# Three passes over rounded parts for the embedding projections of a two-layer decoder step

## What is computed

```python
def run(x, p, sample):
    ...
    for i in range(DEPTH):
        ...
        x = x + rms_norm(m, norm_g[i, 1])
        f = squared_relu_mlp(rms_norm(x, norm_g[i, 2]), w_ff1[i], w_ff2[i])
        x = x + rms_norm(f, norm_g[i, 3])
        gate = jax.nn.sigmoid(x @ w_ple_gate[i] + b_ple_gate[i])
        x = x + gate * (p[i] @ w_ple[i])
```

## Time and profile before

| | |
|---|---|
| runs | 1772.66, 1778.82, 1775.17 us; median 1775.17 us |
| the profiled execution's own time | 1768.82 us |
| its span, first to last instruction | 1767.0 us |
| mean granted clock of TensorE | 0.984 of full |
| PE busy | 1687.0 us, 95% |
| DVE, ACT, POOL busy | 753.2, 621.1, 604.1 us |
| projection's products (L743) | 128 records, 32.4 us busy |
| weight splits on ACT and POOL | 98 each, mean 1907 and 4626 ns |

### The profile page before, as it was taken

One profiled execution on the slowest core, in us unless ns is written; L12 is line 12 of the kernel. 1 busy time (PEld: TensorE's weight loads), 2 busy tenths in 40 slices (PEclk: granted clock), 3 DMA queues, 4 the chain that ended last, 5 costly groups with the idle time before them and its releaser, 6 DMA issues.

```text
span 1767.0 us, 31043 instructions
## 1 busy us (share of the span) xinstructions
PE 1687.0 (95%) x13335; PEld 1575.5 (89%) x13335; DVE 753.2 (43%) x1101; ACT 621.1 (35%) x968; POOL 604.1 (34%) x286
## 2 busy tenths in 40 slices
PE   6999999899999999998999878999799999999998
PEld 6998879799999999997999545668799999999988
DVE  4999953520212112265054757884340111312252
ACT  4211145432322223244222446875343231413232
POOL 3551322233333333322342003665324343333312
PEclk9999999899999999998999998999999999999999
DMA  7229703133322222121336881001212222122212
GB/s 255 80 93 163 240 1 144 72 113 126 131 109 76 93 72 96 48 96 66 91 95 194 290 275 49 2 1 62 96 49 72 80 88 96 72 96 72 84 60 78
DMA packets 61338, 180.07 MB, mean 102 GB/s; under 512 B 22914, under 2 KB 23826, under 8 KB 47314
## 3 DMA queue, kind: packets, MB, share of 16 engines
q1 hardware_dynamic: 60530, 177.18, 30.2%
q10 hardware_dynamic: 128, 0.88, 0.3%
q0 software_dynamic: 544, 0.03, 0.0%
HBM read 167.02 MB, written 16.45 MB: 104 GB/s over the span
## 4 chain that ended last, share of the span: by engine, by line
PE 76%; DVE 15%; ACT 3%; issue 2%; SPq 1%; DMA 1%; POOL 1%; ACTq 0%; DVEq 0%; POOLq 0%
PE ps L691 21%; PE ps L693 21%; PE ps L692 21%; DVE ps L1655 8%; PE ps L1090 2%; PE ps L1080 2%; PE ps L813 2%; PE ps L1107 2%; DVE big L1637 1%; POOL w_lo L615 1%; PE ps L926 1%; DVE hb L1541 1%; ACT w_hi L1147 1%; SPq L531 1%; DVE x L1604 1%
## 5 line engine op out<-in xcount | busy, mean ns | idle before, releaser
L615 POOL TENSOR_TENSOR w_lo<-w_raw,w_hi 128x2048 fp32r<-128x2048 f32 x98 | 453.3, 4626 | 853.5 <-ACT w_hi L1147 853.5
L691 PE MATMUL ps<-ha,w_hi 128*128 128x288 f32 x1920 | 572.4, 298 | 16.5 <-DVE hb L1612 9.1
L692 PE MATMUL ps<-hb,w_hi 128*128 128x288 f32 x1920 | 569.0, 296 | 0.0
L693 PE MATMUL ps<-ha,w_lo 128*128 128x288 f32 x1920 | 568.7, 296 | 0.0
L691 PEld LDWEIGHTS ps<-ha,w_hi 128*128 128x128 f32 x1920 | 363.2, 189 | 23.7 <-issue 17.7
L693 PEld LDWEIGHTS ps<-ha,w_lo 128*128 128x128 f32 x1920 | 363.8, 189 | 0.0
L692 PEld LDWEIGHTS ps<-hb,w_hi 128*128 128x128 f32 x1920 | 363.7, 189 | 0.0
L691 PE MATMUL ps<-hid_hi,w_hi 128*128 128x288 f32 x1024 | 301.8, 295 | 0.0
L693 PE MATMUL ps<-hid_hi,w_lo 128*128 128x288 f32 x1024 | 301.7, 295 | 0.0
L692 PE MATMUL ps<-hid_lo,w_hi 128*128 128x288 f32 x1024 | 301.6, 295 | 0.0
L1147 ACT ACTIVATE w_hi<-w_raw 128x2048 fp32r<-128x2048 f32 x98 | 186.9, 1907 | 174.7 <-PE ps L693 165.1
(11 more groups left out here) (250 smaller groups left out, 1985.0 us busy)
## 6 DMA issues: line engine op xcount, KB each, us to landing
w_raw<-in_w SPq DMA_DIRECT2D x98, 1024.0 KB, 4.8
ring<-in_sel_pages SPq DMA_DIRECT2D x64, 256.0 KB, 3.8
ring<-in_cmp_pages SPq DMA_DIRECT2D x40, 256.0 KB, 4.3
attn_t<-in_win SPq DMA_DIRECT2D x16, 512.0 KB, 7.1
cmp_hb<-in_cmp_pages SPq DMA_DIRECT2D x16, 256.0 KB, 4.3
x<-in_x SPq DMA_DIRECT2D x4, 576.0 KB, 5.9
out_y<-x SPq DMA_DIRECT2D x8, 288.0 KB, 2.1
big<-in_cmp_pages SPq DMA_DIRECT2D x8, 256.0 KB, 4.0
```

Of the source, the lines that this page charges most:

```text
L615: nc.gpsimd.tensor_tensor(w_lo[j % 2][:, :], w_raw[:, k, :], w_hi[j % 2][:, :].bitcast(F32), ALU.subtract).then_inc(w_ready, 1)
L691: nc.tensor.matmul(to, wh, chunk(hi, k, a * HT, HT), start=k == 0, stop=False)
L692: nc.tensor.matmul(to, wh, chunk(lo, k, a * HT, HT), start=False, stop=False)
L693: return nc.tensor.matmul(to, wl, chunk(hi, k, a * HT, HT), start=False, stop=k == C - 1)
```

## The change

The projection's weights become one more stage of the weights' list ("ple0", "ple1", one block each), so that they are split like all others. The embedding input is split into `ple_hi` (ScalarE) and `ple_lo` (VectorE, in place of `ple_in`) in the third quarter of the MLP. TensorE makes 12 products a tile in place of 4. As the helper `tile` now splits the projection's block where it split the gate's first one, and does not act in the projection's own tiles, the gate's first block is split by a call of its own in ScalarE's `ple`, after the copies of tiles 0 and 1. The numbers of the blocks after the projection move by one, so their parity does, and the places in the ring that the attention's transfers use are swapped with them.

```diff
-W_STAGES = ([("pw1", 8), ("pw2", 4)] + [(s, 4) for s, _, _ in mlp_stages(0)] + [("gate0", 4), ("q", 4), ("kv_cmp", 2),
-            ("k_rot", 2), ("v_tok", 2), ("out", 4)] + [(s, 4) for s, _, _ in mlp_stages(1)] + [("gate1", 4)])
+W_STAGES = ([("pw1", 8), ("pw2", 4)] + [(s, 4) for s, _, _ in mlp_stages(0)] + [("ple0", 1), ("gate0", 4), ("q", 4), ("kv_cmp", 2),
+            ("k_rot", 2), ("v_tok", 2), ("out", 4)] + [(s, 4) for s, _, _ in mlp_stages(1)] + [("ple1", 1), ("gate1", 4)])
...
-    _per = TT if _s == "v_tok" else 2
+    _per = TT if _s == "v_tok" else C if _s.startswith("ple") else 2
...
-    if _s.startswith("gate"):
-        BLOCKS.append(("ple", int(_s[-1])))
...
     elif _src == "w1":
-        PLACE.append((BLK, 9))
+        PLACE.append((2 * BLK, 9))
     elif _src == "sel_pages":
-        PLACE.append((BLK * ((_row + 2) % 3), 2 + (_row + 2) % 3))
+        PLACE.append((BLK * (1, 0, 2)[_row % 3], 2 + (1, 0, 2)[_row % 3]))
...
                     if was == "w":
                         sp.wait_ge(w_ready, n + 1)
-                    elif was == "ple":
-                        sp.wait_ge(tile_done, FIRST[f"ple{n}"] + C)
...
             def ple(layer, norm):
 
-                i = B_OF["ple", layer]
-                block_there(i)
-                pe.wait_ge(ple_loaded, 16 * (layer + 1))
-                w = w_raw[:, PLACE[i][1], :].rearrange("p (k c) -> p k c", k=2)
+                j = W_OF[f"ple{layer}"]
+                pe.wait_ge(w_ready, j + 1)
+                pe.wait_ge(ple_split, layer + 1)
+                wh, wl = (w[j % 2].rearrange("p (k c) -> p k c", k=2) for w in (w_hi, w_lo))
...
                         for k in range(2):
-                            last = nc.tensor.matmul(slot(t)[:, a, :], w[:, k, m * P:(m + 1) * P],
-                                                    ple_in[:, k, a * HT:(a + 1) * HT], start=k == 0, stop=k == 1)
+                            columns, tokens = slice(m * P, (m + 1) * P), slice(a * HT, (a + 1) * HT)
+                            nc.tensor.matmul(slot(t)[:, a, :], wh[:, k, columns], ple_hi[:, k, tokens], start=k == 0, stop=False)
+                            nc.tensor.matmul(slot(t)[:, a, :], wh[:, k, columns], ple_lo[:, k, tokens], start=False, stop=False)
+                            last = nc.tensor.matmul(slot(t)[:, a, :], wl[:, k, columns], ple_hi[:, k, tokens], start=False,
+                                                    stop=k == 1)
...
-                if stage in W_OF and m % per == 0:
+                if stage in W_OF and not stage.startswith("ple") and m % per == 0:
...
+                    if n == 2:
+                        act.wait_ge(ple_loaded, 16 * (layer + 1))
+                        nc.scalar.activation(ple_hi[:, :, :], ple_in[:, :, :], ACT.Copy).then_inc(ple_hi_ready, 1)
...
                 out_of(0)
                 out_of(1)
+                split_weight(W_OF[f"gate{layer}"])
                 for m in range(C):
...
+                    if n == 2:
+                        dve.wait_ge(ple_hi_ready, layer + 1)
+                        nc.vector.tensor_tensor(ple_lo[:, :, :], ple_in[:, :, :], ple_hi[:, :, :].bitcast(F32),
+                                                ALU.subtract).then_inc(ple_split, 1)
```

More of the change, by code:

```diff
@@ L125 @@
 HALF = 8
-SIZE = {"w": WB, "w1": BLK, "ple": WB, "cmp_pages": BLK, "sel_pages": BLK, "win_k": BLK // 4, "win_v": BLK // 4}
+SIZE = {"w": WB, "w1": BLK, "cmp_pages": BLK, "sel_pages": BLK, "win_k": BLK // 4, "win_v": BLK // 4}
 B_OF = {b: i for i, b in reversed(list(enumerate(BLOCKS)))}
@@ L143 @@
 for _src, _row in BLOCKS:
-    if _src in ("w", "ple"):
+    if _src == "w":
         PLACE.append((WB * (_raw % 2), _raw % 2))
@@ L247, in program @@
         ple_in = at_byte("ple_in", [P, 2, T], big_byte + 12 * C * T)
+        ple_lo = at_byte("ple_lo", [P, 2, T], big_byte + 12 * C * T, F32R)
+        ple_hi = at_byte("ple_hi", [P, 2, T], big_byte + 12 * C * T + 8 * T, F32R)
         emb = at_byte("emb", [P, C, T], big_byte)
@@ L285, in program @@
         v_cmp_s = big[:, at:at + NB // 2 * 256].rearrange("p (b f) -> p b f", f=256)
-        w1 = at_byte("w1", [P, 2, 16, P], ring_byte + 4 * BLK)
+        w1 = at_byte("w1", [P, 2, 16, P], ring_byte + 8 * BLK)
         assert [PLACE[B_OF["w", W_OF["v_tok"] + v]][0] for v in range(2)] == [WB, 0]
@@ L382, in program @@
         ple_loaded = sem("ple_loaded")
+        ple_hi_ready, ple_split = sem("ple_hi_ready"), sem("ple_split")
         wg_in = sem("wg_in")
@@ L470, in _, with weight_rows @@
             sp.dma_start(par[:, :], ext["par"]).then_inc(consts_in, 16)
+            def weight_rows(j):
+                if j in (W_OF["ple0"], W_OF["ple1"]):
+                    return ext["ple"][int(j == W_OF["ple1"])]
+                return ext["w"][j - (j > W_OF["ple0"]) - (j > W_OF["ple1"])]
             def pair_rows(v):
@@ L508, in _ @@
                         sp.wait_ge(s_mm if src == "win_k" else o_mm, row - 1)
-                if src in ("w", "ple"):
+                if src == "w":
                     to = w_raw[:, k, :]
@@ L537, in _ @@
                     else:
-                        rows = ext["w1"] if src == "w1" else ext[src][row]
+                        rows = ext["w1"] if src == "w1" else weight_rows(row)
                     sp.dma_start(to, rows).then_inc(block_in[k], 16)
```

## The result

The changed kernel is slower: 1784.97 us (median of 7 runs, 1779.36 to 1788.94) against 1775.17 us (7 runs, 1771.97 to 1778.82), a ratio of 1.0057 with a 95% interval of 1.0040 to 1.0074. A second comparison, with 30 runs of the kernel before, gave 1.0042 (1.0021 to 1.0063).

The account below looks back on a forecast made before the run. TensorE's products were taken to set the pace, except in a few handovers. Per layer 3.2 us (held operation, the 0.5 won included) plus 0.7 (clock), twice, gave +7.8 us on 1775.17: 1783.0 us, range 1776 to 1788.

Parts of the forecast that it names:

- The held operation: In each projection, GpSimd's moved weight split delays VectorE's first hb and so the gate: +3.2 us a layer.
- held to the split's end: A VectorE operation with two SBUF inputs starting inside GpSimd's split waits for its end; chunk 0's hb 3.4 us later.
- 759.47 + 3.4 = 762.9, against the old start of 759.73: Layer 0's gate: the copy freeing it comes 3.4 us late, giving +3.2 us a layer.
- the gate is held by TensorE (done at 759.70): Kernel before, layer 0: TensorE holds the gate, the VectorE and ScalarE chain only 0.2 us behind.
- Shorter products: Projection tiles take 1.59 us each, TensorE some 3.4 us less a layer; alone, -0.65 us a layer at the gate.
- -0.5 us: Projection tile 1 ends earlier, so the spread of the norm's factors starts at about 746.6 instead of 747.10.
- The 3.4 us of TensorE's work: TensorE needs some 3.4 us less a layer in the projection, of which only tile 1 lies on the path.
- Rival (c): All of TensorE's saving arrives and the gate starts when the projection is done: 2 x -3.4, 1768.4 us; chance 0.02.
- The clock: TensorE's idle gaps before tiles 6, 7 and the gate may halve its clock: 0 to 2.1 us a layer, 0.7 taken.
- What costs nothing: The embedding's split, the gate's second block and the swapped ring places were taken to add no time.
- (a): In the projection VectorE is not held, so only the shorter products count: 1773.9 us; chance 0.10.
- (b): The clock is half when the gate begins, in both layers: 2 x (3.2 + 2.1), 1785.8 us; chance 0.15.

Follow-up runs that it names:

- e0: The changed kernel run again, unaltered, against the kernel before: ratio 1.0042 (1.0021 to 1.0063).
- e1: The kernel before with only the split of the gate's first weight block moved on ScalarE behind the copy of projection tile 1: ratio 1.0048.
- e2: The changed kernel without GpSimd's subtraction for the first weight block of each gate: ratio 0.9988 to the kernel before.
- e8: The kernel before with two new orders, VectorE's scalings behind the first x and ScalarE's projection copies made earlier: ratio 1.0004.
- e5: The changed kernel with VectorE's scalings right behind the first x and ScalarE's projection copies made earlier: ratio 0.9968 to the kernel before, 1771.1 us against 1775.8.
- e3: The changed kernel with VectorE's new order alone, the seven other scalings right behind the first x: ratio 1.0002 to the kernel before.
- e9: The changed kernel with both new orders, of VectorE and ScalarE, run once more: ratio 0.9965 to the kernel before.
- e4: The changed kernel with ScalarE's new order alone, projection tiles copied as soon as they are done: ratio 1.0053 to the kernel before.

## Why the prediction was right

The forecast was 1783.0 us, slower; measured were 1784.97 and, in e0, 1782.77. The mechanism was as forecast; that the number came so near is in part luck, as two errors in its terms nearly cancel.

- **The held operation.** The step "held to the split's end", for hb of chunk 0, is what the trace shows, and e1 (the move alone costs 1.0048) and e2 (the rest alone, 0.9988) isolate it. Its size was a little small: +3.62 us a layer, not +3.2. GpSimd started 4.30 us after the root, 0.12 later than worked out, and took 4.62, not 4.55; and the step "759.47 + 3.4 = 762.9, against the old start of 759.73" compared a copy with a start. The start follows the copy by 0.26 us in both kernels (759.47 before), so the copy's delay, 3.62, should have been taken whole. Behind this stands a misreading of the kernel before: "the gate is held by TensorE (done at 759.70)". In e8, with the same products and the copy of tile 6 made earlier, the gate starts at 14.23 in place of 14.64, so before it was the copy that held it, by 0.4 us.
- **Shorter products.** "-0.5 us" was 0.34: the copy of tile 1 began 1.77 us after the root in place of 2.11, since the spread came 1.79 us after tile 1's first product, not 1.59. e2's gate, 0.33 us early, is the same number. The 3.4 us of TensorE's work did come free, but as waiting. Rival (c), all of it arriving, did not come true; e5, which no longer makes the gate wait for the copies or for the held hb, starts it 2.6 us earlier than before.
- **The clock.** The 0.7 us a layer was 0 in the profiles of the change and of e0, and 1.6 us in one layer of e1 (5.5 - 3.84). So the two size errors (the held operation 0.4 us a layer too little, the clock 0.7 too much) nearly cancel. How often it falls in unprofiled runs stays open.
- **What costs nothing.** The embedding's split and the ring places: e2, which has them all, is not slower than before. The trace shows the first directly: from the root of the MLP's first norm to that of its last (346.18 to 745.09 before, 350.67 to 749.58 after) layer 0 took 398.91 us in both profiles, and layer 1 the same within 0.01 us. The gate's third tile, forecast to come only 0.1 us behind its block, didn't wait: GpSimd ended 30.5 us after the root and the tile starts at 31.1.
- **Rivals.** (a), VectorE not held, fell by the 4.70 us; (b), half clock in both layers, wasn't seen in the two profiles of the change.

## What to carry to other kernels

When work moves to an engine that was idle in a stretch, look at what the neighbours do in that stretch, not only at the engine's own slack: here 9 us of cover hid GpSimd's 4.6 us from TensorE, and 3.9 us of them came back on VectorE (4.70 for 0.76). If a GpSimd operation that reads SBUF can't be moved, order VectorE so that operations with one SBUF input (the other in PSUM) run beside it; that alone took a loss of 0.4% away (e3), and with ScalarE's copies moved up too it became a gain of 0.3% (e5, e9). And time freed on TensorE counts only when every chain that feeds its next stage is shortened with it: the copies, the input parts and the next weight block each held it in turn (e3, e4, e8).

## What the runs showed that was not expected

The clock's answer to the same gaps isn't the same each time: in one execution of e1 the gate began with 0.94 and 0.50 in layer 0 and at 1.00 in layer 1, after a wait of 2.35 us in both; in e3 it fell in layer 0 alone too, behind a wait of 2.14 us that both layers had. And stages that no edit touched differ by 4 us between executions of one kernel (attention 454.8 and 458.6 us), as much as the effect of one layer, and what makes them differ stays open: only stretches measured from a common event, or many runs, tell such effects apart.
